# Second FFNs of a two-layer hybrid decoder: GpSimd's first low part of each halved pair no longer waits for the third weight sum

## The reference

```python
D_MODEL = 1024
SEQ = 512
DEPTH = 2
D_FF = 2816
def swiglu(x, w1, w3, w2):
    return (jax.nn.silu(x @ w1) * (x @ w3)) @ w2
...
    for l in range(DEPTH):
        x = x + 0.5 * swiglu(rms_norm(x, ffn1_norm[l]), ffn1_w1[l], ffn1_w3[l], ffn1_w2[l])
        h = rms_norm(x, mix_norm[l])
        p = h @ w_in[l]
...
        x = x + merged @ w_out[l]
        x = x + 0.5 * swiglu(rms_norm(x, ffn2_norm[l]), ffn2_w1[l], ffn2_w3[l], ffn2_w2[l])
    return x
```

## Time and profile before

| | us |
|---|---|
| median of 3 runs | 2779.62 |
| lowest and highest | 2779.6, 2779.7 |
| the profiled execution | 2779.76 |
| span of its trace | 2777.7 |
| TensorE busy | 2769.2 (100%) |
| VectorE busy | 1753.7 (63%) |
| ScalarE busy | 1277.0 (46%) |
| GpSimd busy | 853.2 (31%) |

### The profile page before, as it was taken

One profiled execution on the slowest core, in us unless ns is written; L12 is line 12 of the kernel. 1 busy time (PEld: TensorE's weight loads), 2 busy tenths in 40 slices (PEclk: granted clock), 3 DMA queues, 4 the chain that ended last, 5 costly groups with the idle time before them and its releaser, 6 DMA issues.

```text
span 2777.7 us, 41457 instructions
## 1 busy us (share of the span) xinstructions
PE 2769.2 (100%) x15682; PEld 2334.4 (84%) x15682; DVE 1753.7 (63%) x2756; ACT 1277.0 (46%) x1956; POOL 853.2 (31%) x416
## 2 busy tenths in 40 slices
PE   9999999999999999999999999999999999999999
PEld 8888888877788889898988888888777888898988
DVE  5585557685657448585744855576856674585755
ACT  5343344556355446353543423445553553463533
POOL 0075014333333343131100850233333343431321
DMA  5323584222222222232333235732222222223322
GB/s 199 98 91 118 141 152 122 83 74 71 80 88 77 91 94 98 92 114 99 107 129 98 91 129 136 159 107 82 71 76 76 84 84 91 94 90 104 109 95 103
DMA packets 113092, 284.57 MB, mean 102 GB/s; under 512 B 35616, under 2 KB 45344, under 8 KB 112416
## 3 DMA queue, kind: packets, MB, share of 16 engines
q1 hardware_dynamic: 112928, 282.35, 33.2%
HBM read 268.67 MB, written 9.44 MB: 100 GB/s over the span
## 4 chain that ended last, share of the span: by engine, by line
PE 96%; DVE 1%; DMA 1%; SPq 0%; ACT 0%; issue 0%; POOL 0%; DVEq 0%; ACTq 0%
PE bank L594 24%; PE bank L596 24%; PE bank L595 24%; PE bank L678 5%; PE bank L679 5%; PE bank L680 5%; PE bank L622 1%; PE bank L624 1%; PE bank L623 1%; PE bank L988 1%; PE bank L1007 1%; PE bank L1022 1%; PE bank L768 1%; PE bank L1121 1%; PE bank L962 0%; DMA s_ud<-s_uc 0%
## 5 line engine op out<-in xcount | busy, mean ns | idle before, releaser
L464 POOL TENSOR_TENSOR w_lo<-raw,w_hi 128x1024 fp32r<-128x1024 f32 x208 | 519.6, 2503 | 1081.5 <-ACT w_hi L456 1081.5
L594 PE MATMUL bank<-h_hi,w_hi 128*128 128x512 f32 x1840 | 724.1, 394 | 0.4 <-DVE silu_a L2177 0.3
L596 PE MATMUL bank<-h_hi,w_lo 128*128 128x512 f32 x1840 | 716.6, 389 | 0.0
L595 PE MATMUL bank<-h_lo,w_hi 128*128 128x512 f32 x1840 | 716.4, 389 | 0.0
L456 ACT ACTIVATE w_hi<-raw 128x1024 fp32r<-128x1024 f32 x374 | 393.4, 1056 | 565.7 <-PE bank L596 537.5
L594 PEld LDWEIGHTS bank<-h_hi,w_hi 128*128 128x128 f32 x1840 | 345.4, 188 | 78.3 <-issue 7.1
L596 PEld LDWEIGHTS bank<-h_hi,w_lo 128*128 128x128 f32 x1840 | 345.3, 188 | 72.9
L595 PEld LDWEIGHTS bank<-h_lo,w_hi 128*128 128x128 f32 x1840 | 345.6, 188 | 69.5
L464 DVE TENSOR_TENSOR w_lo<-raw,w_hi 128x1024 fp32r<-128x1024 f32 x166 | 230.8, 1390 | 169.9 <-ACT w_hi L456 169.6
L514 POOL TENSOR_TENSOR w_lo<-raw,w_hi 128x1024 fp32r<-128x1024 f32 x80 | 146.6, 1853 | 438.0 <-DVE bank L2228 403.3
L594 PE MATMUL bank<-g_hi,w_hi 128*128 128x512 f32 x698 | 272.1, 390 | 0.2
(11 more groups left out here) (441 smaller groups left out, 5243.0 us busy)
## 6 DMA issues: line engine op xcount, KB each, us to landing
raw<-in_w_lots SPq DMA_DIRECT2D x478, 512.0 KB, 3.5
s_wd<-s_z SPq DMA_DIRECT2D x8, 512.0 KB, 3.8
s_t<-s_taps SPq DMA_DIRECT2D x16, 256.0 KB, 14.0
da_s<-da_qk SPq DMA_DIRECT2D x16, 256.0 KB, 3.8
x<-in_x SPq DMA_DIRECT2D x8, 256.0 KB, 5.9
raw_k<-in_w_lots SPq DMA_DIRECT2D x8, 256.0 KB, 6.1
s_w_re<-s_wd SPq DMA_DIRECT2D x32, 64.0 KB, 3.5
s_w_im<-s_wd SPq DMA_DIRECT2D x32, 64.0 KB, 3.5
```

What stands on the lines that cost most here:

```text
L464: eng.tensor_tensor(w_lo[:, s], raw[:, s], w_hi[:, s].bitcast(f32), SUB).then_inc(S["lo_done"], 1)
L594: pe.matmul(b[:, :], w_hi[:, s, kw], xh[:, k], start=(k == 0), stop=False)
L595: pe.matmul(b[:, :], w_hi[:, s, kw], xl[:, k], start=False, stop=False)
L596: return pe.matmul(b[:, :], w_lo[:, s, kw], xh[:, k], start=False, stop=(k == nk - 1))
```

## The change

One line of GpSimd's program is taken out, a wait that stood in front of the first lot's low part in all 40 halved pairs (20 in each layer). No instruction is added or put elsewhere on any engine.

```diff
@@ -1461,7 +1461,6 @@
                         n = FIRST_LOT[th] + 2 * i
                         if i == PLAIN_PAIRS[th]:
                             pool.wait_ge(S["lo_done"], LOT(n))
-                        pool.wait_ge(S["x7_in_t_sum"], t_at(n, T3))
                         low_of(pool, n)
                         if HALVED[n] == 0:
                             pool.wait_ge(S["gated_done"], G(1) + 1)
```

## The result

The changed kernel takes 2817.85 us (median; 2817.1 to 2818.4) against 2779.61 us before, measured beside it: 1.0136 times as long, 95% interval 1.0124 to 1.0149. That is 38.2 us more; the profiled execution's span grew from 2777.7 to 2816.0, by 38.3. The forecast was 2813.0, with a range of 2804 to 2822: the direction and the range hold, and the size was 4.9 us short. (Behind the change the kernel's lines are numbered one lower: the first weight sum L2226 is now L2225, take_y L2294 is L2293, and so on.)

What follows compares the result with a forecast made beforehand. TensorE, busy 2769.2 of 2777.7 us, was taken as the bound, delayed by VectorE's late take_y. Terms 18.3 + 7.2 + 7.8 = 33.3 us on the profiled run gave 2813.0 us, range 2804 to 2822.

Steps and rivals of the forecast that it cites:

- The bound, the place and the direction: TensorE, busy 2769.2 of 2777.7 us, bounds; late take_y delays q7 in halved pairs; 1.2% slower.
- Exclusion instead of sharing: VectorE operations with two SBUF inputs and GpSimd's w_lo wait for each other to end, 0.55 or 2.25 us after.
- (a): Common pair, 11 per layer: L2226 held, VectorE 1.86 us late, q7 0.83 us later; 22 x 0.83 = 18.3 us.
- (b): Third pair of second and last thirds, 2 per layer: GpSimd first, L2303 held 2.20 us; 4 x 1.81 = 7.2 us.
- (c): Fourth and fifth pairs of the first third, once per layer: two collisions delay take_y; 2 x 3.9 = 7.8 us.
- the variant that was named for it: First layer: GpSimd clears semaphores between lots, so L2278 after take_y is held instead; 3.3 to 3.7 us.
- beyond that slack every delay of take_y is a delay of TensorE: Common pair: take_y is early by 1.08 us for q7; TensorE has no idle time to absorb later delays.
- (d): Remaining 5 pairs per layer, at the starts of the thirds: removing the wait costs nothing.
- The signs: New profile: L2226 near 2.5 us in 22 instances, L2303 or L2274 changed in six, about 26 TensorE waits for take_y.
- the first, that only operations which write SBUF are held: L2226, writing PSUM, passes and L2278 is held: 0.23 us per common pair, 2799.8 us in all; chance 0.06.
- The second, that the slack would swallow it: VectorE wins the port whenever both want it, so only TensorE's two waits can go: 2776.8 us; chance 0.04.
- The third, another engine as the bound: VectorE or ScalarE becomes the bound, each common pair losing 1.2 us more: 2839 us; chance 0.03.

Runs made afterwards that it cites:

- the split operation: The changed kernel with GpSimd's full lot (w_lo) cut into two operations of 512 columns; 2815.09 us, ratio 1.0128.

## Why the prediction was right, and where its sizes were off

**The bound, the place and the direction** were right. TensorE had 8.5 us to give back and lost 38, all at or just behind q7, or q6 ahead of it, in pairs of the second FFNs.

**Exclusion instead of sharing** was right in each number that was read from the earlier trace rows: VectorE's operation of 512 columns ends 0.55 to 0.56 us after GpSimd's, GpSimd's ends 2.25 to 2.27 us after VectorE's, an operation of 256 columns 0.28 after GpSimd, as estimated (L2302: 1083.96 against 1083.68, rows below), and operations with a PSUM input pass.

**(a), 22 common pairs.** L2225 was to be 1.86 us late and is 1.88. The slack came as foretold too. The term that was mis-sized is what a wait costs beside its length: 0.94 us per pair against 0.83. About 0.10 of it lies behind the wait. Before, TensorE's matmuls followed each other every 0.12 us, and q7's first weight load started 0.12 us ahead of its matmul (1106.14, 1106.26); after the wait both start at 1112.78, and the second matmul only 0.22 us later (1113.00). 22 x 0.94 = 20.7 us against 18.3.

**(b), 4 pairs.** That GpSimd would be first was a guess on 0.06 us, and it came true by luck as much as by reading: GpSimd is issued first, by 0.07, and L2302 is the one held (third pair of the second third, compare):

```profile
1190.93 2.40 POOL L514 TENSOR_TENSOR w_lo<-raw,w_hi 128x1024 fp32r<-128x1024 f32 x1 [4.32 <-ACT w_hi L509]
...
1191.00 2.62 DVE L2302 TENSOR_TENSOR gated<-gated,rstd 128x256 f32<-128x256 f32 x1
```

From the first sum before it to the first sum behind, 20.06 us against 18.17 in the kernel before: 1.89 against 1.81, again the 0.1 us of the restart. 4 x 1.89 = 7.6 against 7.2.

**(c), the start of the first third.** This was the largest error: 4.9 us in the first layer (from the first sum at 1052.57 to the one at 1094.18, 41.61 against 36.69 before) and, read the same way, 5.25 in the second, 10.2 against 7.8. In the first layer it went by the variant that was named for it: since GpSimd clears semaphores between its lots, not L2273 but L2277 behind it was held:

```profile
1072.52 2.69 POOL L514 TENSOR_TENSOR w_lo<-raw,w_hi 128x1024 fp32r<-128x1024 f32 x1 [1.34 <-DVE g_lo L2277]
...
1073.49 2.26 DVE L2277 TENSOR_TENSOR g_lo<-gated,g_hi 128x512 fp32r<-128x512 f32 x1
...
1081.30 2.38 POOL L514 TENSOR_TENSOR w_lo<-raw,w_hi 128x1024 fp32r<-128x1024 f32 x1 [2.40 <-ACT w_hi L509]
1081.36 2.60 DVE L2302 TENSOR_TENSOR gated<-gated,rstd 128x256 f32<-128x256 f32 x1
```

In the second layer L2273 is held, 2.89 us. The two collisions are as foretold, and TensorE stops 3.50 us at q7. Up to there the size was right as well: from the first sum of the lot to that q7 it is 3.60 us more than before in the first layer (3.3 to 3.7 was said for this variant) and 3.93 in the second (3.96 was said), though the wait of the pair before is partly one for copy_x at q6. The step that failed is "beyond that slack every delay of take_y is a delay of TensorE": behind this stop another 1.3 us per layer are added, by the 14 or 15 matmuls at half the clock. By the earlier trace rows TensorE had no stop over 1.4 us in this code before, but asking what TensorE's clock does after such a stop would have been due as soon as 3.9 us stood in the sum.

The Trainium skill (TensorE: Matmul & The Clock Gate, section "What's actually happening") does say that an idle TensorE loses its clock, and the rows above agree. Where the clock will fall these runs don't settle: it did in one of two equal stops of 2.1 us.

**(d), ten places,** cost nothing, measured alone as 0.4 us within an interval of about 2.5 to each side.

**The sum** is 20.7 + 7.6 + 10.2 = 38.5 us, where the span grew by 38.3. Against the forecast's terms that is 2.4 us more in (a), 0.4 in (b) and 2.4 in (c).

**The signs.** Of those named, nearly all came: L2225 at 2.57 us in exactly 22 instances, L2302 at 2.60 to 2.62 in six. Two more are held that the count of "six" had left out, though its own text had two collisions for each start, L2277 once and L2273 once; so 30 of the 40 places collide and ten don't. The other signs: GpSimd's releaser is w_hi, and TensorE's list has 29 waits where "about 26" were expected. The distance from q1 to q7 was to be 9.4 us and is 1112.78 - 1103.32 = 9.46. **The rivals:** the first, that only operations which write SBUF are held, falls twice: by the 2.57 us of a sum that writes PSUM, and by the kernel in which that same sum, with an input in PSUM, is not held. The second, that the slack would swallow it, falls by 29 waits. The third, another engine as the bound, is not what the change does, but it is near: with take_y moved, VectorE sets the pair's length at 10.73 us, 0.26 below the 10.99 of the change.

## What to carry to other kernels

A wait that protects no data may be a schedule: here it keeps a 2.4 us GpSimd operation away from a row of VectorE operations with two SBUF inputs each and lays it over those that read PSUM, and it is worth 38 us, all of it in 30 of its 40 places. Before such a wait is removed or moved, list what the other engine runs in the following 2.5 us by where its *inputs* lie, and how much slack the last of its users has; a held operation showed as a long duration and a higher busy share (58 us more with the same instructions), not as idle time, so look for it in min/median/max of single lines. When a forecast adds up to a stop of TensorE longer than any that the trace of before shows there, ask what its clock does afterwards.

## What the runs showed of the hardware

A wait of TensorE cost about 0.10 us more than its length, since the matmul behind it started 0.22 us after the first in place of 0.12.

The granted clock fell to 0.50 around or just behind TensorE's stops of 3.50 and 3.51 us in every trace that has them, and in the traces it stayed at 1.00 after every stop of up to 1.9 us. In between the same length went both ways within one execution: 2.14 us without a fall and 2.13 with one (the kernel with take_y moved), and 3.17 us with a fall and 3.16 without (the split operation). So no length at which the clock falls can be read from these runs. How many matmuls went at half clock was not the same each time either: 14 to 17 in most places, 28 and 24 in the kernel with only the first third's two places changed. Why it differs stays open.

In the split kernel the two engines alternated when both had operations with two SBUF inputs queued: in no pair that was looked at was one of them kept out for more than one operation of the other, in either direction.
